# A fused hybrid encoder layer: projection stages reordered, recurrent gates on four quarters of the array

## What is computed

```python
u = rms(x, norm1_g)
q, k, v, x_lru, g_lru = split(u @ w_in, 5)                 # five parts of 512 columns
out_sb = stick_breaking(q, k, v)                           # 8 heads x 64, causal
xc = causal_dwconv(x_lru, conv_w, conv_b)                  # 4 taps
r = sigmoid(xc @ w_rgate + b_rgate)                        # block diagonal: 8 blocks of 64x64
i = sigmoid(xc @ w_igate + b_igate)
a = exp(8 * r * log_sigmoid(lam)); s = sqrt(1 - a**2) * i * xc
h[t] = a[t] * h[t-1] + s[t]
out_lru = h * gelu(g_lru)
y = x + concat(rms(out_sb), rms(out_lru)) @ w_out
return rms(y + hier_moe(rms(y)), final_g)                  # 32 experts, 2 per token
```

## Time and profile before

| | |
|---|---|
| median of 3 runs | 4645.36 us |
| profiled execution | 4648.48 us, span 4646.4 us |
| TensorE busy | 92% of the span |
| QKV stage | 0 to 634 us |
| LRU stage | 635 to 1151 us |
| attention and the rest | from 1152 us |

### The profile page before, as it was taken

One profiled execution on the slowest core, in us unless ns is written; L12 is line 12 of the kernel. 1 busy time (PEld: TensorE's weight loads), 2 busy tenths in 40 slices (PEclk: granted clock), 3 DMA queues, 4 the chain that ended last, 5 costly groups with the idle time before them and its releaser, 6 DMA issues. The chain is left out here.

```text
span 4646.4 us, 85418 instructions
## 1 busy us (share of the span) xinstructions
PE 4282.4 (92%) x28496; PEld 3206.5 (69%) x28497; DVE 2892.6 (62%) x3384; ACT 2518.9 (54%) x3914; POOL 605.7 (13%) x771
## 2 busy tenths in 40 slices
PE   6999979996999998999996999938999999999998
PEld 5878767774555555555554888837888878888886
DVE  3222245665998998999995333375656555555665
ACT  3222224444787887888885323213656555555665
POOL 0000002221000000000000000021223232222322
PEclk9999989998999999999998999969999999999999
DMA  4222231111201102001002333334656555554663
GB/s 136 90 100 104 85 120 54 54 52 41 91 29 52 34 29 63 22 29 63 4 9 79 143 138 130 123 127 147 247 204 245 199 207 197 192 205 169 247 246 141
DMA packets 279572, 539.95 MB, mean 116 GB/s; under 512 B 38321, under 2 KB 103857, under 8 KB 279345
## 3 DMA queue, kind: packets, MB, share of 16 engines
q1 hardware_dynamic: 228512, 410.49, 25.0%
q0 software_dynamic: 46224, 118.03, 7.3%
q10 hardware_dynamic: 4608, 8.39, 0.5%
HBM read 410.97 MB, written 176.16 MB: 126 GB/s over the span
## 5 line engine op out<-in xcount | busy, mean ns | idle before, releaser
L945 DVE TENSOR_TENSOR_SCAN att_R<-att_stay,att_R 128x512 f32<-128x512 f32 x896 | 1058.9, 1261 | 25.8 <-ACT att_stay L885 23.5
L895 ACT ACTIVATE att_RT<-att_rt 128x512 f32<-128x512 f32 (+3 forms) x1152 | 585.8, 562 | 234.0 <-PE att_rt L836 204.5
L836 PEld LDWEIGHTS att_rt<-ident,att_R 64*128 64x128 f32 x8448 | 319.8, 139 | 372.0 <-issue 368.3
L885 ACT ACTIVATE att_stay<-att_z 128x1024 f32<-128x1024 f32 (+2 forms) x576 | 555.5, 965 | 25.2 <-PE att_z L823 23.7
L849 PE MATMUL att_out<-att_RT,att_dv 128*64 128x512 f32 (+3 forms) x2304 | 521.9, 574 | 0.0
L836 PE MATMUL att_rt<-ident,att_R 64*128 64x64 f32 x8448 | 384.0, 227 | 98.5 <-ACT att_RT L895 53.4
L1257 DVE TENSOR_TENSOR ew_lo<-ew_raw,ew_hi 128x1024 fp32r<-128x1024 f32 x372 | 430.1, 1218 | 13.6 <-ACT ew_hi L1250 13.6
L1250 ACT ACTIVATE ew_hi<-ew_raw 128x1024 fp32r<-128x1024 f32 x384 | 373.8, 1047 | 97.3 <-PE ex_down L1680 97.3
L243 PE MATMUL qkv_out<-qkv_u_hi,qkv_w_hi 128*128 128x512 f32 x768 | 308.8, 402 | 18.2 <-DVE qkv_u_lo L234 18.2
L243 PE MATMUL qkv_out<-qkv_u_hi,qkv_w_lo 128*128 128x512 f32 x768 | 303.4, 395 | 0.0
L243 PE MATMUL qkv_out<-qkv_u_lo,qkv_w_hi 128*128 128x512 f32 x768 | 300.9, 392 | 0.0
(11 more groups left out here) (262 smaller groups left out, 8430.6 us busy)
## 6 DMA issues: line engine op xcount, KB each, us to landing
ew_raw<-in_w_e_gate SPq DMA_DIRECT2D x32, 2048.0 KB
ew_raw<-in_w_e_up SPq DMA_DIRECT2D x32, 2048.0 KB
ew_raw<-in_w_e_down SPq DMA_DIRECT2D x32, 2048.0 KB
qkv_x<-in_x SPq DMA_DIRECT2D x32, 512.0 KB, 5.0
lru_x<-in_x SPq DMA_DIRECT2D x32, 512.0 KB, 4.9
mix_raw<-s_mix_t SPq DMA_DIRECT2D x32, 512.0 KB, 4.1
mix_x<-in_x SPq DMA_DIRECT2D x32, 512.0 KB, 4.8
s_h<-mix_h SPq DMA_DIRECT2D x32, 512.0 KB, 3.5
```

Source lines behind the costliest of these rows:

```text
L836: last = nc.tensor.transpose(rt[half][:, h, qt, :], R[lanes, n % 3, h, qt, s * P:(s + 1) * P], k.ident[lanes, lanes])
L885: done = nc.scalar.activation(pair(stay[:, step % 4, :]), pair(z[step % 2][:]), ACT.Sigmoid, scale=-scale)
L895: nc.scalar.activation(RT[:, :, s, first:, half, :], rt[half][:, :, first:, :], ACT.Copy).then_inc(rt_copied[half], 1)
L945: nc.vector.tensor_tensor_scan(R[:, n % 3, h, s, 0:width][:, ::-1], src[:, ::-1], src[:, ::-1], initial, ALU.mult, ALU.bypass).then_inc(sc ...
```

## The change

In both stages TensorE's, ScalarE's and VectorE's orders are rewritten. The first two transposes of group G + 1 stand inside the last product of group G, behind its first four chunks, and the high and low parts of these two chunks are made before ScalarE and VectorE turn to that last product; chunks 2 to 7 are made at the head of the next group. In `qkv` the transposes of dv are spread, four behind each of the products q1, q2, q3 and k0, and staging and storing follow the same order. In `lru` a gate call for one block of channels (`pe_gates`) issues four matmuls of 64x64 weights, one for each quarter of the array; the i gate's halves come out exchanged and ScalarE's sigmoid puts them back with two instructions of 64 partitions. The calls stand behind g0, within g1, behind g1 and within g2. Decays and roots of the group before go between the x copies, the sigmoids before the gelus, and VectorE's factors and scans between and behind the convolutions. The scan has a buffer of its own. The gate buffer holds only the 64x64 blocks, and is no longer cleared. The last group is written out behind each TensorE loop.

```diff
-self.junk = sb(tag + "junk", [P, D])
+self.junk = None if normed else sb(tag + "junk", [P, D])
...
-    def leading_products(self, pe, G, banks, weights, cols, done):
+    def first_transposes(self, pe, G):
...
+    def leading_products(self, pe, G, banks, weights, cols, done):
...
+    def pe_dv(pe, G, j):
+        pe.wait_ge(dv_ready, G * NP + j + 1)
+        pe.wait_ge(dv_staged, G * NP + j + 1)
+        for b in range(TT):
...
+    def pe_group(pe, G, last):
+        pe.wait_ge(qk_low, G * 8 + LEAD)
+        ug.leading_products(pe, G, out[:LEAD], weights, [2 * W_SB + j * P for j in range(LEAD)], v_done)
+        for j in range(LEAD, NP):
+            pe.wait_ge(qk_low, G * 8 + j + 1)
+            ug.product(pe, G, out[j], weights, 2 * W_SB + j * P, range(DC)).then_inc(v_done, 1)
+        for j in range(NP):
+            pe.wait_ge(v_copied, G * NP + j + 1)
+            ug.product(pe, G, out[j], weights, j * P, range(DC)).then_inc(qk_done, 1)
+            if j > 0:
+                pe_dv(pe, G, j - 1)
+        for j in range(NP):
+            pe.wait_ge(qk_low, G * 8 + j + 5)
+            if j < NP - 1:
+                ug.product(pe, G, out[j], weights, W_SB + j * P, range(DC)).then_inc(qk_done, 1)
+            else:
+                ug.product(pe, G, out[j], weights, W_SB + j * P, range(DC // 2))
+                if not last:
+                    ug.first_transposes(pe, G + 1)
+                ug.product(pe, G, out[j], weights, W_SB + j * P, range(DC // 2, DC)).then_inc(qk_done, 1)
+            if j == 0:
+                pe_dv(pe, G, NP - 1)
...
     def _(pe):
...
+        ug.first_transposes(pe, 0)
+        with pe.Fori(0, NG - 1) as G:
+            pe_group(pe, G, False)
+        pe_group(pe, NG - 1, True)
...
-    def act_group(act, G, last):
+    def stage_dv(act, G, j):
...
+    def act_group(act, G, first, last):
+        if not first:
+            ug.high(act, G, range(2, DC))
...
-        for m in range(4):
+        for m in range(7):
...
+            if 0 < m <= NP:
+                stage_dv(act, G, m - 1)
...
-            ug.high(act, G + 1)
+            ug.high(act, G + 1, range(2))
+        split_high(act, G, 7)
...
-    def dve_group(dve, G, last):
+    def dve_group(dve, G, first, last):
+        if not first:
+            ug.low(dve, G, range(2, DC))
...
-        for m in range(8):
+        for m in range(7):
...
-            ug.low(dve, G + 1)
+            ug.low(dve, G + 1, range(2))
+        split_low(dve, G, 7)
...
+    def store_dv(sp, G, j):
...
-        for m in range(4):
+        for m in range(8):
...
+            if 0 < m <= NP:
+                store_dv(sp, G, m - 1)
...
-gates = sb("lru_gates", [P, 2, NL, P])
+gates = sb("lru_gates", [P, 2, NL, HD])
...
-    h = r
+    h = sb("lru_h", [P, NL, GT])
...
-    gate_done = sem("lru_gate_done")
+    gate_done = [sem(f"lru_gate_done{n}") for n in range(2)]
...
+    def half_of(half):
+        return slice(half * HD, (half + 1) * HD)
...
-        sp.wait_ge(cleared, 1)
...
-                sp.dma_start(gates[lanes, n, :, 64 * half:64 * half + 64],
+                sp.dma_start(gates[lanes, n, :, :],
...
+    def pe_gates(pe, G, j):
+        pe.wait_ge(xc_ready, G * NL + j + 1)
+        hold(pe, k, r_ready, G * NL + j + 1)
+        hold(pe, k, i_ready, G * 2 * NL + 2 * j + 2)
+        for n in range(2):
+            for half in range(2):
+                lanes, there = half_of(half), half_of(half ^ n)
+                nc.tensor.matmul(gate_out[n][there, :], gates[lanes, n, j, :], xc[lanes, 1, j, :],
+                                 start=True, stop=True).then_inc(gate_done[n], 1)
+    def pe_group(pe, G, last):
+        pe.wait_ge(g_ready, G * NL + LEAD)
+        ug.leading_products(pe, G, out[:LEAD], weights, [j * P for j in range(LEAD)], x_done)
+        for j in range(LEAD, NL):
+            pe.wait_ge(g_ready, G * NL + j + 1)
+            ug.product(pe, G, out[j], weights, j * P, range(DC)).then_inc(x_done, 1)
+        for j in range(NL):
+            pe.wait_ge(x_copied, G * NL + j + 1)
+            ug.product(pe, G, out[j], weights, W_LRU + j * P, range(DC // 2))
+            if j in (1, 2):
+                pe_gates(pe, G, 2 * j - 1)
+            if j == NL - 1 and not last:
+                ug.first_transposes(pe, G + 1)
+            ug.product(pe, G, out[j], weights, W_LRU + j * P, range(DC // 2, DC)).then_inc(g_done, 1)
+            if j in (0, 1):
+                pe_gates(pe, G, 2 * j)
...
+    def sigmoids(act, G):
...
         for j in range(NL):
...
+            act.wait_ge(gate_done[0], G * 2 * NL + 2 * j + 2)
...
-            act.wait_ge(gate_done, G * 2 * NL + 2 * j + 2)
+            act.wait_ge(gate_done[1], G * 2 * NL + 2 * j + 2)
...
+            for half in range(2):
+                lanes, there = half_of(half), half_of(1 - half)
+                nc.scalar.activation(ig[lanes, j, :], gate_out[1][there, :], ACT.Sigmoid,
+                                     bias=k.b_i[lanes, j:j + 1]).then_inc(i_ready, 1)
+    def act_group(act, G, first, last):
+        if not first:
+            ug.high(act, G, range(2, DC))
+        for j in (0, 1):
+            copy_x(act, G, j)
+        if not first:
+            decays(act, G - 1)
+        copy_x(act, G, 2)
+        if not first:
+            roots(act, G - 1)
+        copy_x(act, G, 3)
+        sigmoids(act, G)
+        if first:
+            act.wait_ge(slope_ready, 1)
+        if last:
+            decays(act, G)
+            roots(act, G)
+            for j in range(NL):
+                gelu_of(act, G, j)
+        else:
+            for j in range(NL - 1):
+                gelu_of(act, G, j)
+            ug.high(act, G + 1, range(2))
+            gelu_of(act, G, NL - 1)
+    def decays(act, G):
...
+    def roots(act, G):
...
+    def convolve(dve, G, blocks):
+        for j in blocks:
...
-        if not last:
-            ug.scale(dve, G + 1)
+    def gated_inputs(dve, G):
         for j in range(NL):
-            dve.wait_ge(i_ready, G * NL + j + 2)
+            dve.wait_ge(i_ready, G * 2 * NL + 2 * j + 4)
...
-    def dve_tail(dve, G):
+    def factors(dve, G):
...
+    def recurrence(dve, G):
...
+            dve.wait_ge(g_ready, G * NL + j + NL + 1)
...
+    def dve_group(dve, G, first, last):
+        if not first:
+            ug.low(dve, G, range(2, DC))
+        convolve(dve, G, (0, 1))
+        if not first:
+            factors(dve, G - 1)
+        convolve(dve, G, (2, 3))
+        if not first:
+            recurrence(dve, G - 1)
+        if not last:
+            ug.scale(dve, G + 1)
+        gated_inputs(dve, G)
+        if not last:
+            ug.low(dve, G + 1, range(2))
...
-        dve.sem_inc(i_ready, 1)
+        dve.sem_inc(i_ready, 2)
...
+        factors(dve, NG - 1)
+        recurrence(dve, NG - 1)
...
     def _(pool):
-        nc.gpsimd.memset(gates[:], 0.0).then_inc(cleared, 1)
...
```

More of the change, by code:

```diff
@@ L342, in _ @@
             @block.tensor
             def _(pe):
-                with pe.Fori(0, NG) as G:
-                    pe.wait_ge(qk_low, G * 8 + LEAD)
-                    ug.leading_products(pe, G, out[:LEAD], weights, [2 * W_SB + j * P for j in range(LEAD)], v_done)
-                    for j in range(LEAD, NP):
-                        pe.wait_ge(qk_low, G * 8 + j + 1)
-                        ug.product(pe, G, out[j], weights, 2 * W_SB + j * P, range(DC)).then_inc(v_done, 1)
-                    for j in range(NP):
-                        pe.wait_ge(v_copied, G * NP + j + 1)
-                        ug.product(pe, G, out[j], weights, j * P, range(DC)).then_inc(qk_done, 1)
-                    for j in range(NP):
-                        pe.wait_ge(dv_ready, G * NP + j + 1)
-                        pe.wait_ge(dv_staged, G * NP + j + 1)
-                        for b in range(TT):
-                            last = nc.tensor.transpose(dv_tr[j % 2][:, b * P:(b + 1) * P],
-                                                       dv[:, j, b * P:(b + 1) * P], k.ident[:])
-                        last.then_inc(dv_transposed, 1)
-                    for j in range(NP):
-                        pe.wait_ge(qk_low, G * 8 + j + 5)
-                        ug.product(pe, G, out[j], weights, W_SB + j * P, range(DC)).then_inc(qk_done, 1)
@@ L551, in _ @@
                 pe.wait_ge(gates_loaded, 64)
-                with pe.Fori(0, NG) as G:
-                    pe.wait_ge(g_ready, G * NL + LEAD)
-                    ug.leading_products(pe, G, out[:LEAD], weights, [j * P for j in range(LEAD)], x_done)
-                    for j in range(LEAD, NL):
-                        pe.wait_ge(g_ready, G * NL + j + 1)
-                        ug.product(pe, G, out[j], weights, j * P, range(DC)).then_inc(x_done, 1)
-                    for j in range(NL):
-                        pe.wait_ge(x_copied, G * NL + j + 1)
-                        ug.product(pe, G, out[j], weights, W_LRU + j * P, range(DC)).then_inc(g_done, 1)
-                    for j in range(NL):
```

(36 more changed lines are left out.)

64 lines of the change are left out of this document (24 added, 40 removed).

## The result

The changed kernel takes 4587.5 us, the median of four executions (4583.2 to 4590.8), against 4646.0 for the kernel before: a ratio of 0.9873, 95% interval 0.9856 to 0.9890. That is 58.5 us less; the forecast was 4576 us, 69.1 less. A second set of runs gave 4587.4 against 4648.6, 0.9871 (0.9856 to 0.9886), 61.3 us less.

A forecast was written before the change was run, and what follows sets the result against it. TensorE, busy 92% of the span, was taken to bound the kernel; savings of 10.9 + 11.5 + 5.3 + 29.9 + 11.5 = 69.1 us from 4645.4 gave 4576 us, with an 8-in-10 range of 4566 to 4610.

The forecast's parts named there:

- the narrower 4567 to 4590: Whole kernel: the forecast's own range in us around 4576, given a chance of 0.70.
- The heads: QKV and LRU group seams: first transposes inside the previous product save 10.9 and 11.5 us.
- The cover: After the moved transposes, 12 matmuls (2.75 us) hide the wait for the first chunk's low half, ready 1.2 us early.
- dv's transposes: QKV: spreading them between products saves 0.66 us in each of 8 groups, 5.3 us.
- The gate calls: LRU: four overlapping 64x64 quarters, 1.10 us a call, save 4.27 us at 7 seams, 29.9 us.
- LRU's end: Last group's first matmul to the next stage's first load: 69.8 instead of 81.3 us, saving 11.5 us.
- Pairs: Rival, LRU gate calls: row halves sharing a PSUM bank take turns, 0.86 us more a call, 4604 us; chance 0.15.
- Heads not hidden: Rival, QKV and LRU seams: late copies bring the heads back, 22.4 us lost, 4598 us; chance 0.08.
- one after another: Rival, LRU gate calls: quarters don't overlap, 3.68 us a call, kernel slower at 4659 us; chance 0.05.
- the drain: Gate-call borders: 0.16 us for both mode changes taken; a half-pass's tail at each border would make 0.32.
- The margin of the sigmoids: LRU: sigmoids ready 3.1 us after a gate call starts, next call at 3.9 us, margin 0.8 us.

The follow-up runs named there:

- the kernel with the heads back: Changed kernel with the two first transposes and their splits back at each group's head in QKV and LRU: 4610.0 us.
- the kernel that does run in pairs: Changed kernel with the i gate on the same two diagonal quarters as the r gate: 4615.7 us.
- the double call: Changed kernel with chunk c+2's transpose between the two banks' products of chunk c, and two blocks' gates per call: 4576.5 and 4578.1 us.
- the kernel with the quarters alone: Kernel before, both stages in its old order, with only the gate tiles and halved i-gate sigmoids new: 4718.3 us, ratio 1.0149.

## Why the prediction was right, and where it was off

The mechanisms and all signs were right, and the time lies in the range, 11.5 us above the forecast. The terms account for 4.9 of these 11.5, and no run explains the rest. That the time lies even within the narrower 4567 to 4590 is in part luck. Term by term, by periods:

1. *The heads.* 1.56 and 1.65 us a seam were forecast; 1.49 and 1.60 came, as the kernel with the heads back measures them. The cover held: no wait of TensorE at a head remains. (0.07 + 0.05) x 7 = 0.8 us short over both stages.
2. *dv's transposes.* 0.66 forecast, 0.62 measured: 0.3 us short over eight groups.
3. *The gate calls.* This is the step that was mis-sized: 1.10 us forecast, 1.21 measured, so 3.8 us a group instead of 4.27. The assumption that all four quarters overlap was right. The borders were too cheap. 0.86 for the streaming and 0.16 for both changes of mode make 1.02, and 1.02 is what lies between the first half-pass and the product; but the step into the call is 0.09 us longer as well, and the restart is 0.10 instead of 0.08. The prediction read attention's calls from their first half-pass on. What stands in front of that row, in the trace of the kernel before, has such a step too:

```profile
1566.04 0.69 PE L836 MATMUL att_rt<-ident,att_R 64*128 64x64 f32 x16
```

The last single record of these sixteen starts at 1566.508, the first half-pass of the call at 1566.661: 0.15 us, where the transposes follow one another by 0.03. So the missing 0.1 us could have been read there. Over the seams, 0.45 us a group x 7 = 3.2 us.
4. *LRU's end.* 69.8 us forecast, 70.4 measured. The chain behind the last sigmoid took the 23.8 us of the forecast; up to there it was 46.6 instead of 46: three calls of 0.11 more, the last call and its sigmoids 3.25 instead of 3.1 (1060.77 to 1064.02), and the rest is rounding.

Together, 0.8 us in QKV (0.07 x 7 + 0.04 x 8) and 0.5 x 7 + 0.6 = 4.1 in LRU, 4.9 in all: the stages gave 64.2 of 69.1. The remaining 3 to 6 us, down to the medians' 61.3 and 58.5, are no term of the sum. The forecast was made by subtracting from one median what one execution's rows gave, and both kernels vary by some microseconds in attention, mixing and the first groups. Whether the changed kernel is on average a little slower there, or the few executions fell so, stays open.

One reading of the prediction was wrong and moved no term. It has the granted clock at 9 or more tenths through slices 1 to 10; the earlier trace rows shows 8 in slices 6 and 10. In the trace of before the lower clock lies there at the start of the LRU stage (0.50 from 633.5 to 657.0 us) and in its end, where TensorE has no work (0.50 from 1131.7 to 1150.0); a steady group has 1.00, and the row of the clock is the same after the change.

The rivals. *Pairs* fell twice: the records of the four quarters start 6 to 7 ns apart, and the kernel that does run in pairs takes 1.87 us a call. The Trainium skill (TensorEngine Tiling (Array Packing), Gotcha 1: PSUM Pressure), by which different row tiles can't access the same PSUM bank at once, is not borne out for row halves that write different lanes of a bank: with the bank shared or not, a call took 1.02 us. *Heads not hidden* fell with the missing waits, *one after another* with the first records of a call.

On the drain the trace stands between the two values that the prediction weighed. Against two half-passes in line, 0.86, the quarters' 1.02 and the 0.09 in front make 0.25 us a call at the borders, between attention's row (0.16) and a half-pass's tail at both (0.32). The Trainium skill (TensorEngine Tiling (Array Packing), Tiling Modes) has a drain there. What a border costs with all that goes with it, the restart included, is what the double call saves, 0.34 us a call; how much of that is a drain no run shows.

The margin of the sigmoids was forecast at 0.8 us and is 0.73, which one more half sigmoid of 0.70 just used up. There a lost margin cost its wait alone. What the prediction didn't see is that waits for the sigmoids can cost more: in the kernel with the quarters alone, where they are 3.17 us long and a call of 1.09 us stands between them, they also cost the clock.

## What to carry to other kernels

A faster form of a small step is worth its streaming time less its borders, and only where it doesn't wait for its consumer in between: here four quarters at the end of a group were 71 us slower than before, and the same quarters between long products 58 to 61 us faster, of which the order by itself brings 44. Put several such calls together if the banks are there (0.34 us for each call saved). Make the sum by periods of steady groups, and don't read a difference of 3 us from the median of four executions when an unchanged stage varies by 6.

## What the runs showed of the hardware

**The clock fell where TensorE waited 3.17 us behind a short call.** In the kernel before, one gap of 1.06 us in the gates and one of 1.29 at the head left it at 1.00. In the kernel with the quarters alone, one call of 1.09 us and one wait of 3.17 us stood before its fall, and one more such call: in the group shown above the clock fell at about the end of the second call, before the second wait was over, and the same eight half-passes then took 1.98 us. In the next group the second call was slow already:

```profile
913.18 1.98 PE L570 MATMUL lru_gate_out<-lru_xc,lru_gates 64*64 64x512 f32 x8 [3.17 <-ACT lru_ig L591]
```

**VectorE's convolutions slow down beside GpSimd.** Two timelines of the changed kernel, VectorE's and GpSimd's:

```profile
871.86 2.33 DVE L699 SCALAR_TENSOR_TENSOR lru_xc<-lru_xl,conv_w,lru_xc 128x512 f32<-128x512 f32 x3
...
875.60 4.30 DVE L699 SCALAR_TENSOR_TENSOR lru_xc<-lru_xl,conv_w,lru_xc 128x512 f32<-128x512 f32 x3
...
885.24 4.15 DVE L699 SCALAR_TENSOR_TENSOR lru_xc<-lru_xl,conv_w,lru_xc 128x512 f32<-128x512 f32 x3
```

```profile
874.22 5.14 POOL L811 TENSOR_TENSOR lru_sq<-lru_a 128x512 f32<-128x512 f32 x4 [39.69 <-ACT lru_a L669]
881.68 6.38 POOL L815 TENSOR_TENSOR lru_sq<-lru_th,lru_ig 128x512 f32<-128x512 f32 x4 [2.32 <-ACT lru_th L678]
```

A block's three taps alone take 2.33 us, beside GpSimd's products 4.30 and 4.15. With the second product cut to 16 columns, VectorE's timeline has, for blocks 1 and 2:

```profile
875.67 4.30 DVE L699 SCALAR_TENSOR_TENSOR lru_xc<-lru_xl,conv_w,lru_xc 128x512 f32<-128x512 f32 x3
...
883.25 2.33 DVE L699 SCALAR_TENSOR_TENSOR lru_xc<-lru_xl,conv_w,lru_xc 128x512 f32<-128x512 f32 x3
```

The Trainium skill (SBUF — State Buffer, SBUF: two separate sides) has this as an exclusive lock on a port pair that GpSimd and a VectorE operation with two SBUF inputs share; the trace agrees. Each slowed tap takes about as long as a product of GpSimd's beside it (1.41 to 1.67 us, against 1.18 to 1.75), and each of the five ends 0.55 us after such a product has ended (block 1's at 877.01, 878.46 and 879.91, GpSimd's at 876.47, 877.91 and 879.36). The sixth, behind GpSimd's last product, takes 0.75 us. Here it lies under TensorE's products and costs nothing: with the short product the LRU groups stay 53.5 us apart.
